# A recurrent layer whose gates run in eight steps beside its input projection, with both directions in turn and the gelu half kept on chip

## What is computed

```python
def recurrent_block(h, w_in, conv_w, conv_b, w_a, b_a, w_x, b_x, lam, w_out):
    z = h @ w_in                                   # 1024 -> 3072
    xr, gate = jnp.split(z, 2, axis=-1)
    xr = centred_depthwise_conv(xr, conv_w, conv_b)   # 4 taps over the tokens
    y = (rg_lru(xr, w_a[0], b_a[0], w_x[0], b_x[0], lam[0], reverse=False)
         + rg_lru(xr, w_a[1], b_a[1], w_x[1], b_x[1], lam[1], reverse=True))
    y = y.astype(h.dtype) * jax.nn.gelu(gate)
    return y @ w_out

def rg_lru(x, w_a, b_a, w_x, b_x, lam, reverse):
    r = sigmoid(blockwise x @ w_a + b_a)           # 16 blocks of 96 x 96
    i = sigmoid(blockwise x @ w_x + b_x)
    log_a = -LRU_C * r * softplus(-lam)
    a = exp(log_a)
    u = sqrt(-expm1(2.0 * log_a)) * (i * x)
    h[t] = a[t] * h[t-1] + u[t]                    # or from the last token to the first
```

## Time and profile before

| what | us |
|---|---|
| median of 3 runs | 3534.59 |
| the three runs | 3533.22, 3534.59, 3539.70 |
| the profiled execution, its own time | 3521.77 |
| the span of its trace | 3520.1 |

### The profile page before, as it was taken

One profiled execution on the slowest core, in us unless ns is written; L12 is line 12 of the kernel. 1 busy time (PEld: TensorE's weight loads), 2 busy tenths in 40 slices (PEclk: granted clock), 3 DMA queues, 4 the chain that ended last, 5 costly groups with the idle time before them and its releaser, 6 DMA issues.

```text
span 3520.1 us, 36607 instructions
## 1 busy us (share of the span) xinstructions
PE 3058.4 (87%) x15338; PEld 1354.6 (38%) x15338; DVE 858.9 (24%) x1276; ACT 499.0 (14%) x983; POOL 236.1 (7%) x336
## 2 busy tenths in 40 slices
PE   7998878598999999999598899998799507999998
PEld 3465555232323333333246444444233203444443
DVE  2324242311211111111134300013320851201003
ACT  1031131000000000000013300002002930100001
POOL 0000011211011011011100000000100320000000
PEclk8989978799999999999799999999899758999999
DMA  7108941789999999999541212211220031312210
GB/s 263 48 7 306 358 139 41 289 321 404 389 403 406 400 401 404 404 402 391 232 168 44 82 48 95 94 67 53 57 65 25 14 71 30 113 48 95 85 58 24
DMA packets 167017, 646.18 MB, mean 184 GB/s; under 512 B 20091, under 2 KB 29883, under 8 KB 126257
## 3 DMA queue, kind: packets, MB, share of 16 engines
q1 hardware_dynamic: 151138, 605.91, 44.8%
q0 software_dynamic: 13872, 34.89, 3.4%
q10 hardware_dynamic: 1856, 3.21, 0.3%
HBM read 630.11 MB, written 18.38 MB: 184 GB/s over the span
## 4 chain that ended last, share of the span: by engine, by line
PE 49%; issue 32%; DMA 5%; DVE 5%; POOL 3%; PEld 2%; ACT 2%; POOLq 2%; DVEq 1%; PEldq 0%; ACTq 0%; SPq 0%
PE ps L2221 13%; PE ps L2232 13%; PE ps L2349 6%; PE ps L2525 3%; PE ps L2006 2%; DMA stage<-gate_dram 2%; DMA slots<-in_ada_w_dram 2%; PE ps L2171 2%; PE ps L1104 2%; POOLq L1536 2%; PE ps L314 1%; POOL work L1545 1%; PEld ps L434 1%; PE ps L245 1%; DVE slots L2494 1%
## 5 line engine op out<-in xcount | busy, mean ns | idle before, releaser
L1645 PE MATMUL ps<-slots,hT 128*32 128x512 f32 x5120 | 581.4, 599 | 25.8 <-issue 9.4
L2221 PE MATMUL ps<-hT,slots 128*128 128x512 f32 x1024 | 448.6, 599 | 13.1 <-issue 6.6
L2232 PE MATMUL ps<-slots,work 128*128 128x512 f32 x1024 | 441.8, 593 | 12.2 <-DVE work L2269 12.2
L1645 PEld LDWEIGHTS ps<-slots,hT 128*32 128x32 f32 x5120 | 160.8, 110 | 422.4 <-issue 407.2
L2221 PEld LDWEIGHTS ps<-hT,slots 128*128 128x128 f32 x1024 | 195.1, 192 | 265.7 <-issue 265.7
L2232 PEld LDWEIGHTS ps<-slots,work 128*128 128x128 f32 x1024 | 193.7, 190 | 258.8 <-issue 247.6
L1681 PE MATMUL ps<-slots,work 128*32 128x512 f32 x2112 | 253.7, 606 | 27.8 <-DMA slots<-in_w_down_dram 20.0
L2349 PE MATMUL ps<-hT,slots 128*96 128x512 f32 x512 | 223.3, 597 | 26.6 <-DVEq L2355 24.8
L2525 PE MATMUL ps<-slots,work 96*128 96x512 f32 x256 | 112.6, 602 | 107.2 <-DVE work L2512 107.2
L1796 DVE TENSOR_SCALAR stage<-ps 128x512 f32<-128x512 f32 (+1 forms) x47 | 32.2, 686 | 589.3 <-PE ps L1647 588.9
L1681 PEld LDWEIGHTS ps<-slots,work 128*32 128x32 f32 x2112 | 90.2, 111 | 158.6 <-issue 126.6
(11 more groups left out here) (542 smaller groups left out, 2891.8 us busy)
## 6 DMA issues: line engine op xcount, KB each, us to landing
slots<-in_w_up_dram SPq DMA_DIRECT2D x128, 2048.0 KB, 18.0
slots<-in_w_down_dram SPq DMA_DIRECT2D x64, 2048.0 KB, 16.4
slots<-in_mlp_w_dram SPq DMA_DIRECT2D x32, 2048.0 KB, 8.7
slots<-in_ada_w_dram SPq DMA_DIRECT2D x16, 2048.0 KB, 9.5
slots<-in_w_ada_dram SPq DMA_DIRECT2D x12, 2048.0 KB, 8.3
slots<-in_ada_w_dram SPq DMA_DIRECT2D x16, 1024.0 KB, 7.1
slots<-in_rnn_w_in_dram SPq DMA_DIRECT2D x8, 1536.0 KB, 7.1
slots<-in_w_in_dram SPq DMA_DIRECT2D x5, 2048.0 KB, 13.1
```

Source lines behind the costliest of these rows:

```text
L1645: ins = pe.matmul(to, x[:, k, unit * UNIT:(unit + 1) * UNIT], upw[s][:, k % 2, col:col + CH], start=k == 0, stop=False)
L2221: ins = pe.matmul(ps[:, m], slots[:, s, k, m * P:(m + 1) * P], hT[:, k, :], start=k == 0, stop=k == KT - 1)
L2232: ins = pe.matmul(ps[:, 4 + 2 * (t % 2) + h], h1T[:, k, t * P:(t + 1) * P], slots[:, 2 + h, k], start=k == 0, stop=k == KT - 1)
```

## The change

- The three stages become one: `rnn_pe`, `rnn_act`, `rnn_pool`, `rnn_dve`, without the barriers. `rnn3_pe` remains.
- The projection runs in eight groups of four blocks, in the order `RX`: x0, x1, x2, z0, x3, z1, z2, z3. Each of the groups from the second on is a `step`, in which the gate products of one unit stand between its blocks (two units in the fifth group).
- Units alternate direction: unit `k` is block group `k // 2`, direction `k % 2`. The forward result stays in `yfw` until the backward one of the same blocks is added, straight into `xr`.
- Gate products use banks 4 to 7, two blocks at a time, where they had all eight; projection blocks keep banks 0 to 3.
- Two sets of `decays`, `inputs` and `mults` in place of three, in slots 3 to 5. The square root of a unit is taken right after its own exp, not one unit later.
- The gelu of a `z` group is taken in two pairs into `zg` (half of it per block) before and after the square root of a unit; DVE multiplies it into `xr` from there. `gate_dram` and its 16 writes and 16 reads are gone.
- Projection weights come in slots 0 to 2 in turn; the output weights in slots 2 to 5; gate weights come by four blocks and both directions, four small loads each, in two buffers (`wg`), issued on POOL's queue.
- DVE gives the first four `bank_free` ahead of its wait for the small parameters.
- The loads of the second MLP no longer wait for `gated`.

The diff, cut to its core:

```diff
+        RX = ("x", 0), ("x", 1), ("x", 2), ("z", 0), ("x", 3), ("z", 1), ("z", 2), ("z", 3)
...
-            for h in range(2):
-                for s in range(4):
-                    take(pe, s)
-                    for m in range(4):
...
+            def gates(k, m):
+                b, d = k // 2, k % 2
+                if m == 0:
+                    pe.wait_ge(S(f"wg_in{b % 2}"), 64 * (b // 2 + 1))
+                    pe.wait_ge(S("bank_free"), before("bank_free", "r") + 4 + (b + 1) * BB)
+                if k * BB + m >= 2:
+                    pe.wait_ge(S("gate_read"), k * BB + m - 1)
+                for j in range(2):
+                    ins = pe.matmul(ps[0:RW, 4 + 2 * (m % 2) + j], wg[b % 2][:, d, j, m], xr[:, b * BB + m], start=True, stop=True)
+                ins.then_inc(S("gate_ps"), 1)
...
+            def step(i, unit, second_unit=None):
+                gates(unit, 0)
+                gates(unit, 1)
+                take(pe, i % 3)
+                block(i, 0)
+                gates(unit, 2)
+                gates(unit, 3)
+                block(i, 1)
+                if second_unit is not None:
+                    gates(second_unit, 0)
+                    gates(second_unit, 1)
+                block(i, 2)
+                if second_unit is not None:
+                    gates(second_unit, 2)
+                    gates(second_unit, 3)
+                block(i, 3)
...
+            for m in range(BB):
+                block(0, m)
+            pe.drain().then_inc(freed[0], 1)
+            step(1, 0)
+            step(2, 1)
+            step(3, 2)
+            step(4, 3, 4)
+            step(5, 5)
+            step(6, 6)
+            step(7, 7)
...
-            v.wait_ge(S("rnn_in"), NRIN)
             v.nop().then_inc(S("bank_free"), 4)
+            v.wait_ge(S("rnn_in"), NRIN)
...
+            def gelus(b, pair):
+                for i in range(2):
+                    n = b * BB + 2 * pair + i
+                    a.wait_ge(S("product"), before("product", "r") + RX.index(("z", b)) * BB + 2 * pair + i + 1)
+                    if n >= 2:
+                        a.wait_ge(S("gated"), n - 1)
+                    a.activation(zg[:, i], ps[0:RW, 2 * pair + i], ACT.Gelu_apprx_tanh).then_inc(S("z_read"), 1)
...
+            for b in (1, 2):
+                conv(4 * b)
+                gate_in(b - 1)
+                conv(4 * b + 1)
+                one_minus(b - 1)
+                conv(4 * b + 2)
+                scans(b - 1)
+                conv(4 * b + 3)
+            gate_in(2)
+            one_minus(2)
+            gated(0, 0)
+            scans(2)
+            gated(0, 1)
+            conv(12)
+            gate_in(3)
+            conv(13)
+            one_minus(3)
+            conv(14)
+            scans(3)
+            gate_in(4)
+            conv(15)
+            one_minus(4)
+            scans(4)
+            for b in (1, 2):
+                gate_in(b + 4)
+                one_minus(b + 4)
+                gated(b, 0)
+                scans(b + 4)
+                gated(b, 1)
+            gate_in(7)
+            one_minus(7)
+            scans(7)
+            gated(3, 0)
+            gated(3, 1)
...
-                rnn_pe(pe); end()
-                rnn2_pe(pe); end()
+                rnn_pe(pe)
                 rnn3_pe(pe)
```

More of the change, by code:

```diff
@@ L2383, in build @@
-        BB = 4
-        NBAT = 2 * RB // BB
-        def four(a):
-            return a[0:RW].rearrange("p (m t) -> p m t", m=BB)
-        flat = [slots[:, i].rearrange("p k n -> p (k n)") for i in range(6)]
-        decays = [four(flat[0][:, 0:2048]), four(flat[1][:, 0:2048]), four(flat[5][:, 0:2048])]
-        inputs = [four(flat[0][:, 2048:4096]), four(flat[1][:, 2048:4096]), four(flat[5][:, 2048:4096])]
-        mults = [four(flat[3][:, 0:2048]), four(flat[3][:, 2048:4096]), four(work[:, 11264:13312])]
@@ new lines, in rnn_gate_loads, with block @@
+        def rnn_gate_loads(sp, b):
+            for d in range(2):
+                for j, name in enumerate(("rnn_w_a_2", "rnn_w_x_2")):
+                    sp.dma_start(wg[b % 2][:, d, j], A[name][0, d, b * BB:(b + 1) * BB].rearrange("n i j -> i n j")).then_inc(S(f"wg_in{b % 2}"), 16)
+        def rnn_pe(pe):
+            def block(i, m):
+                part, b = RX[i]
+                if i and RX[i - 1][0] == "z":
+                    pe.wait_ge(S("z_read"), TT + RX[i - 1][1] * BB + m + 1)
+                else:
+                    pe.wait_ge(S("bank_free"), before("bank_free", "r") + 4 + (RX[i - 1][1] * BB + m + 1 if i else 0))
+                for k in range(KT):
+                    ins = pe.matmul(ps[0:RW, m], slots[:, i % 3, k, m * RW:(m + 1) * RW], hT[:, k, :], start=k == 0, stop=k == KT - 1)
+                ins.then_inc(S("product"), 1)
+            def gates(k, m):
[8 more added lines that the diff above has]
+                ins.then_inc(S("gate_ps"), 1)
+                if m == BB - 1 and d:
+                    pe.drain().then_inc(S("wg_free"), 1)
+            def step(i, unit, second_unit=None):
[14 more added lines that the diff above has]
+                block(i, 3)
+                pe.drain().then_inc(freed[i % 3], 1)
+            turned(pe, "b", TT - 1)
+            take(pe, 0)
+            for m in range(BB):
[8 more added lines that the diff above has]
+            step(7, 7)
@@ new lines, in rnn_dve @@
+            for n in range(4):
+                conv(n)
+            for b in (1, 2):
[14 more added lines that the diff above has]
+            conv(13)
@@ L2519, in product @@
                 for h in range(2):
[L2520 to L2523 removed]
                     for n in range(RB):
[L2525 removed]
+                        if t == 0 and n % 8 == 0:
+                            take(pe, RO_SLOT[h][n // 8])
+                        ins = pe.matmul(ps[:, 2 * (t % 2) + h], xr[:, n, t * P:(t + 1) * P], slots[0:RW, RO_SLOT[h][n // 8], n % 8], start=n == 0, stop=n == RB - 1)
                     ins.then_inc(S("product"), 1)
```

258 lines of the change are left out of this document (110 added, 148 removed).

## The result

| | median, us | runs | range, us | profiled execution, us | its span, us | granted clock |
|---|---|---|---|---|---|---|
| before | 3535.12 | 4 | 3533.22 to 3539.70 | 3521.77 | 3520.1 | 0.929 |
| after | 3370.74 | 4 | 3367.06 to 3377.70 | 3372.02 | 3370.4 | 0.947 |

The profiled execution of before is not one of its four runs, the one of after is. The ratio is 0.9546, with a 95% interval of 0.9525 to 0.9566: 164.4 us less. The forecast was 3376 with a range of 3358 to 3402.

A forecast was written before the change was run, and what follows sets the result against it. It took PE's queue as the merged stage's floor: 223.5 + 55.0 + 1.9, plus 13.8 for stops and restarts and 7.1 at the end, made 301.3 us against 459.8, so 3534.6 - 158.5 = 3376 us, range 3358 to 3402.

The forecast's parts named there:

- queue's floor: PE's work in the merged stage without stops: projection 223.5, gate products 55.0, first group 1.9, together 280.4 us.
- first stop: PE waits 3.3 us at the first gate product, after x0, for convolutions held back by late parameters and decay parameters.
- second stop, unit 4: In the fifth group PE waits 2.7 us at unit 4's third gate pair for ACT's sigmoids.
- third stop, unit 5: PE waits 2.4 us at the third gate pair of unit 5, taken to cost no restart.
- restarts: PE works at its lower clock after a stop: 2.7 us, taken twice, 5.4 us in all.
- end piece: The last unit's chain and last gelus end 7.1 us after PE's last projection block.
- output weights, slot 4: Load issued 4.5 us before the output products, landing in time: costed at nothing, up to 5 us if diluted.
- The convolutions beside POOL: DVE's convolutions, with one input in PSUM, were taken as not slowed by POOL's squares: cost nothing.
- rival of slower convolutions: DVE slower in the mixed stage: convolutions half again or twice as long, time 3390 or 3402 us; chance 0.20.
- never stops: PE stops only the first time in the merged stage: 293.5 us, a time of 3368; chance 0.15.
- The queues did not lock: Rival that in-order queues lock and each unit's chain holds PE: only 84 us gained, 3451; chance 0.03.
- the clock held at 0.97: Against the rival that stops drop PE's clock, running the mixed queue at half rate: 3655 us; chance 0.02.

The follow-up runs named there:

- a_all: Changed kernel with an x1 block before the first gate products, unit 5's later gates delayed, last group's gates, root and gelus rearranged: 3348.60 us, stage 283.2.
- a_wait_back: Changed kernel with the wait for the small parameters put back ahead of the first bank_free: 3389.27 us, stage 317.4 against 300.6.
- after_again: The changed kernel as it is, profiled and timed again: 3369.39 us, ratio to before 0.9548, stage 300.6 us.
- a_tanh_twice: Changed kernel with every unit's four tanh computed twice on ACT: stage 303.3 us against 300.6.
- a_pe_order5: Changed kernel with the second half of unit 5's gate products one block later in PE's queue: 3370.09 us, stage 293.4 against 300.6.

## Why the prediction was right, and where it was not

| step of the prediction | forecast, us | measured, us |
|---|---|---|
| queue's floor (projection, gates, first group cold) | 280.4 | 281.5 (a_all: 283.2 less 0.3 at the start and 1.4 at the end) |
| first stop | 3.3 | 3.45 |
| second stop, unit 4 | 2.7 | none |
| third stop, unit 5 | 2.4 | 5.06 |
| restarts | 5.4 | 1.7 + 2.1 = 3.8 |
| end piece | 7.1 | 6.69 |
| stage | 301.3 | 300.6 |
| gain of the early start | 16.6 | 15.6 and 16.8 in the stage, 16.4 and 16.7 at PE's first product |
| output weights, slot 4 | 0 | no wait of PE on a load |
| from the output product on | unchanged | 590.8 against 591.2 |

**The stage** is right to 0.7 us, but not each term of it. The step "Second and third stop" put 2.7 us on unit 4 and 2.4 on unit 5, and the trace has nothing on the one and 5.06 on the other. For unit 4 I had ACT at its sigmoids at 2640, which is 2649.9 in this execution (its stage began 9.9 us later), and PE waiting for their first pair, 1.3 us, from 2648.5 on. ACT came 1.3 us earlier, at 2648.59, and PE 1.4 us later, at 2649.90, so that two small errors took the whole 2.7 away. The lateness was made one unit later: by the scans of unit 3 behind convolution 14, and by POOL's squares meeting two DVE instructions of 2048 elements, which the earlier trace rows would have told me to count, since they have two SBUF inputs as line 2494 has. The sum, 8.5 against 8.4 us, is a coincidence of two errors, not a success of the method. Elsewhere too errors cancel: the restarts were taken 1.6 us too long and the queue's floor 1.1 us too short.

**The first stop** has its size for a reason that I named wrongly. In the changed kernel the parameters are ready at 2498.9, and three convolutions later, at 2508.56, the fourth begins just as PE's last block ends; both limits fall on the same 0.1 us (DVE, the last step of the parameters and the fourth convolution):

```profile
2498.84 0.18 DVE L2484 TENSOR_SCALAR modB<-modB 96x32 f32<-96x32 f32 x1
...
2508.56 0.81 DVE L2489 TENSOR_SCALAR work<-ps,modB 96x512 f32<-96x512 f32 x1
```

a_wait_back separates them, and the stop stays. Whoever had hastened the parameters by this prediction would have gained nothing in this execution, and 0.4 us in that of after_again, where they landed 0.4 us later and the stop was 3.82 us.

**The restarts** were 1.7 and 2.1 us where I took 2.7. The third stop was held free of a restart because it was shorter than any in the rows that cost one. The trace has no stop of that length there, but the reason was wrong: in a_tanh_twice 1.9 us of idle time cost 1.7, as much as 3.45 did.

**The convolutions beside POOL** were counted as not slowed, and are not. Convolutions 5, 9 and 13 ran beside the squares, and the first half of 15. By line, min/median/max in ns, of the changed kernel:

```profile
L2491 DVE SCALAR_TENSOR_TENSOR work<-ps,modB,work x16: 744/745/746, 2499.8 to 2666.9; 96x510 f32<-96x510 f32 x16
L2500 DVE TENSOR_TENSOR slots<-slots,work x8: 2286/2288/2929, 2528.9 to 2753.3; 96x2048 f32<-96x2048 f32 x8
L2506 DVE SCALAR_TENSOR_TENSOR slots<-stage,slots x16: 676/1096/1520, 2537.7 to 2760.6; 96x512 f32<-96x512 f32 x16
L2471 POOL TENSOR_TENSOR stage<-slots x16: 1031/1037/3084, 2533.7 to 2759.0; 96x512 f32<-96x512 f32 x16
```

With one input in PSUM the spread is 2 ns over all sixteen; with two in SBUF an instruction takes up to 1520 in place of 676 ns, and POOL's up to 3084 in place of 1031. That closes the rival of slower convolutions. The Trainium skill's rule for the port pair ("SBUF — State Buffer", section "SBUF: two separate sides") foretold which instructions would meet. It says that the later one is fully blocked, and the lengths fit that if a length holds the wait: L2500 grows by 0.64 us, less than one square (1.03), and a square by 2.05 us, less than one L2500 (2.29). The trace does not show the lock itself.

**The other rivals.** PE stops, so "never stops" fell, by one stop only; its 293.5 us is what a_pe_order5 measured (293.4). The queues did not lock, and the clock held at 0.97: the stops are few because three blocks, 20.8 us, stand between most of the gate products.

**The time itself.** The forecast was 3376 against a median of 3370.74. The stage explains 0.7 us of the 5.3. Against the profiled execution I had said 3363.3, and it took 3372.0; there the stage began 9.9 us later than in the one of before, which is the program ahead of it. Between the medians the gain was 164.4 us in one comparison and 156.4 in another, around the 159.2 of the stage. So the remaining 4.6 us lie outside the stage and have both signs; a cause for them was not looked for.

## What to carry to other kernels

Two stages that are bound by different engines can be laid over each other, and the time is then the floor of the busiest queue plus its stops; work out that floor first, here 280.4 us, and measure each order against it. For a stop, read backwards through the engines that are not the bound, to the instruction that waits with ready work queued behind it, and mend the order there or move the waiting engine's request one block later. A cause that explains a wait's size may still not be its cause, where two limits end at the same time: move one of them, and see.

## What the runs showed of the chip

- A stop of PE of 1.16 us had no restart (3.67 us for four products), and one of 1.41 none either; 1.87 and 1.90 cost 1.7 us each, 3.45 cost 1.7, 5.06 cost 2.1, and 5.05 in two other executions 1.7 and 2.7. Before the output product 6.7 us of idle time cost 1.9 to 3.5 us in different executions, and the 107.23 us of the kernel before 2.2 (57.36 against 55.20). The price follows no simple line in the length of the stop.
- After a stop of 1.87 us (a_tanh_twice) the granted clock was 1.00 for the first 1.3 us and 0.50 only then, so it fell while PE was already at work again.
- DVE's convolution steps, with one PSUM input, keep their time beside POOL to 2 ns in 745; those with two SBUF inputs take up to 2.2 times theirs, and POOL's up to 3.0 times.
